# Which kind of expert unit follows which, and in what pieces the first weight blocks arrive: one change to a hybrid SSD, attention and MoE layer

## The chip, the core and the metric

The kernel runs on one core of a Trainium2 chip, as one launch. The metric is the device time in microseconds. The kernel before was timed three times: 1325.1, 1325.3 and 1327.98 us, a median of 1325.3 us. All numbers of the profile come from one further execution of it, which took 1323.47 us, with a span of 1321.8 us between its first and last instruction.

## What is computed

One layer of a streaming encoder over 512 tokens of width 1024, all in f32. The part that matters here is the end, the mixture of experts, and the very beginning, the first projection:

```python
mod = jax.nn.silu(c) @ ada_w[i] + ada_b[i]
sh1, sc1, g1, sh2, sc2, g2 = [m[:, None, :] for m in jnp.split(mod, 6, axis=-1)]
n1 = rms_norm(h, norm1_g[i]) * (1.0 + sc1) + sh1
proj = n1 @ w_in[i]            # 1024 x 6160; then SSD, banded attention, gates, w_out
...
# MoE: 64 experts (gate and up 1024x256, down 256x1024), 6 of them for each token
combine = ...                  # tokens x 64, normalised top-6 weights times 2.5
out = (jax.nn.silu(n @ s_gate) * (n @ s_up)) @ s_down
for e in range(N_EXPERTS):
    hid = jax.nn.silu(n @ e_gate[e]) * (n @ e_up[e])
    out = out + (hid @ e_down[e]) * combine[:, e:e + 1]
...
h = h + g2 * ff                # then the final rms_norm
```

Each of the 64 experts has 3 MB of weights (three transfers of 1024 KB), so the expert stage reads 192 MB.

## The kernel before

**The stages.** The input projection comes first (weights pass as blocks of 1024x256 through `ring`, a ring of four slots), then SSD, attention, the two branch projections and the gates, the output projection, the router, and the expert stage. The instructions of each engine stand in a fixed order that is written out by hand; semaphores tie the engines together.

**The first projection.** TensorE works on the first six outputs of the projection side by side (`OUTER`, 6 PSUM banks), K tile by K tile: for K tile k it does outputs 0 to 2, then the preparation of tile k+1 (`next_tile`: two tiny products of the adaLN sum of that tile, four transposes of x), then outputs 3 to 5. Outputs 0 and 1 use block 0, outputs 2 and 3 block 1, outputs 4 and 5 block 2. The preparation of a tile needs VectorE's `modulation_sum`, which in turn needs that tile's 1 MB of `ada_w` (`load_chunk`, two transfers of 512 KB). All of this is loaded by the one queue of SyncE (SP): chunk 0, the four tiles of x, then chunk 1, block 0, chunk 2, block 1, and so on.

**The expert stage.** Experts are sorted by their number of tokens on the chip. Experts 0 to 3 (`FIXED`) are taken out of the sort: their weights are loaded before the routing is known, and they are done first. The other 60 follow by rank, the fullest first. Work goes in units. In a single unit one expert has up to 128 token rows; in a pair unit two experts have 64 rows each, one in the upper and one in the lower half of the PE array's columns. The 16 fullest ranked experts (4 to 19) are singles, the rest come in pairs. The order of units before: 4 fixed singles; then 16 times single, pair; then, in a loop whose count depends on the routing (`LAST`), 6 pairs. That is 42 units here.

**Slots.** The weights sit in six slots (`gu(s)` for gate and up, `dn(s)` for down). The n-th expert in the order of use goes to slot n % 6, which the expert used six before it has left. Slots 4 and 5 first hold the normed tokens and the shared expert's weights, so their first expert loads wait for the shared expert (`sgu_ready`, `sy_ready`) and for the first gather (`gathered[0]`). SP issues each later load in the same order: it reads the expert's number from `order`, waits until the gate and up product of the slot's user is through (`gu_ready`), issues gate and up, waits until its down product is through (`ey_ready`), issues down. `unit_of` and `rank_of` turn positions into units and ranks.

**A unit on TensorE.** Gate and up (`gate_up`, line 1713), the transposes of the next unit's gathered tokens (line 1701), the down product of the unit before (`down`, line 1721), the transposes of this unit's hidden rows (line 1728). GpSimd gathers each unit's tokens from DRAM and scatters its results (lines 653 and 661) on a queue of its own; it fills one half of the row numbers from the token lists and VectorE the other (`upper`, lines 1254 and 1255).

## Time and profile before

| what | value |
|---|---|
| median of three runs | 1325.3 us |
| the profiled execution: its time, and its span | 1323.47 us, 1321.8 us |
| busy share of the span: TensorE, weight loads, VectorE, ScalarE, GpSimd | 91%, 47%, 36%, 19%, 15% |
| moved by DMA in all | 322.28 MB, mean 244 GB/s |
| SP's queue (q1), GpSimd's queue (q0) | 269.37 MB, 47.30 MB |
| first expert unit starts, last down product ends | 714.55 us, about 1270.2 us |

A busy share of 91% for TensorE hides two stretches of another kind: the first 40 us, and the expert stage from 887 us on, where it waits before many units. The rows below show them. "Idle before" in square brackets is the time that the engine stood still before the instruction, and what ended it; "issue" stands where no releaser is seen. Several instructions of a group that follow each other are merged to one row with a count. An f32 product appears as two records.

### The profile page before, as it was taken

What the parts mean: (1) busy time and instruction counts of PE and PEld (TensorE: products, weight loads), DVE (VectorE), ACT (ScalarE), POOL (GpSimd) and SP (SyncE); (2) the same over time, 40 slices, a digit from 0 to 9 for tenths busy, and PEclk for the clock granted to TensorE, in tenths of its full rate; (3) what the DMA queues carried; (4) which work ended last, traced back from release to release, by engine and by line L of the source; (5) the groups of instructions that cost most, each with busy time, mean ns of one, the idle gap of its engine ahead of it and who ended that gap; (6) DMA issues with size and microseconds to landing.
All of it is one profiled execution on the core that took longest, in us unless ns stands there. A gap on an engine that the chain in (4) does not pass through costs nothing. (4 is left out here: it accounts for less than half of the span.)

```text
span 1321.8 us, 13412 instructions
## 1 busy us (share of the span) xinstructions
PE 1203.9 (91%) x4819; PEld 619.1 (47%) x4819; DVE 471.5 (36%) x981; ACT 250.6 (19%) x615; POOL 195.9 (15%) x321
## 2 busy tenths in 40 slices
PE   3999999998999999999998999999898899978866
PEld 1545865465544444448843544433343343433322
DVE  4567035555566111113754222221222222221125
ACT  2141122133441000001122211121111111111101
POOL 4000021111002000000252122221121211111100
PEclk9999999999999998999999999999999998999988
DMA  9633232123448241137247689999999999999747
GB/s 303 179 96 95 64 128 84 61 79 128 141 131 302 64 159 32 64 105 327 80 160 271 250 337 400 422 423 421 422 411 403 410 393 410 391 406 422 306 184 288
DMA packets 108010, 322.28 MB, mean 244 GB/s; under 512 B 14405, under 2 KB 67737, under 8 KB 80937
## 3 DMA queue, kind: packets, MB, share of 16 engines
q1 hardware_dynamic: 87728, 269.37, 53.0%
q0 software_dynamic: 18688, 47.30, 10.0%
q10 hardware_dynamic: 1528, 4.77, 0.9%
q8 instruction: 38, 0.62, 0.2%
q14 instruction: 28, 0.22, 0.1%
HBM read 314.49 MB, written 26.82 MB: 258 GB/s over the span
## 5 line engine op out<-in xcount | busy, mean ns | idle before, releaser
L1713 PE MATMUL ps<-gu_hi,xsT 128*64 128x512 f32 (+1 forms) x672 | 218.4, 616 | 19.9 <-DMA gu_hi<-in_exp_w_up_dram 11.6
L1713 PEld LDWEIGHTS ps<-gu_hi,xsT 128*64 128x64 f32 (+1 forms) x672 | 84.7, 164 | 133.0 <-issue 130.6
L1271 DVE SCALAR_TENSOR_TENSOR hid<-ps,wgt,gated 128x256 f32<-128x256 f32 x42 | 20.3, 484 | 316.2 <-ACT gated L880 316.2
L1591 PE MATMUL ps<-n1T,ring 128*128 128x512 f32 x256 | 112.4, 600 | 3.7 <-DVE mod L1121 3.0
L1713 PE MATMUL ps<-gu_lo,xsT 128*64 128x512 f32 (+1 forms) x352 | 94.1, 652 | 23.1 <-issue 19.4
L1374 PE MATMUL ps<-n1T,ring 128*128 128x512 f32 x256 | 111.9, 594 | 0.0
L1721 PE MATMUL ps<-dn_hi,hidT 128*64 128x512 f32 (+1 forms) x336 | 108.6, 596 | 0.0
L661 POOL DMA_INDIRECT expert_rows<-hn,meta x42 | 41.9, 997 | 420.0 <-DVE hn L1267 397.1
L1267 DVE TENSOR_TENSOR hn<-ps,g_row 128x1024 f32<-128x1024 f32 x42 | 51.4, 1225 | 94.8 <-PE ps L1721 94.8
L1591 PEld LDWEIGHTS ps<-n1T,ring 128*128 128x128 f32 x256 | 49.1, 193 | 65.2 <-issue 61.3
L880 ACT ACTIVATE gated<-ps 128x256 f32<-128x256 f32 x42 | 16.1, 384 | 334.8 <-PE ps L1713 334.8
L1374 PEld LDWEIGHTS ps<-n1T,ring 128*128 128x128 f32 x256 | 48.1, 190 | 58.7 <-issue 58.7
L1382 PE MATMUL ps<-ring,n1T 128*128 128x256 f32 x320 | 70.3, 380 | 0.0
L870 ACT ACTIVATE xsT<-ps,mod 128x128 f32<-128x128 f32 x172 | 64.8, 457 | 26.2 <-PE ps L1701 26.2
L1713 PEld LDWEIGHTS ps<-gu_lo,xsT 128*64 128x64 f32 (+1 forms) x352 | 33.4, 154 | 75.3 <-issue 75.1
L1382 PEld LDWEIGHTS ps<-ring,n1T 128*128 128x128 f32 x320 | 60.5, 190 | 9.2 <-issue 1.2
L1721 PEld LDWEIGHTS ps<-dn_hi,hidT 128*64 128x64 f32 (+1 forms) x336 | 38.7, 160 | 47.8 <-issue 46.4
L1261 DVE TENSOR_SCALAR xsT<-ps,mod 128x128 f32<-128x128 f32 x172 | 58.8, 404 | 5.5 <-PE ps L1701 5.5
L1564 PE MATMUL ps<-xbcT,ring 128*128 128x512 f32 x128 | 58.4, 599 | 0.0
L1619 PE MATMUL ps<-ring,raw 128*128 128x256 f32 x256 | 56.6, 380 | 1.8 <-DVE raw L1111 1.8
L1701 PEld LDWEIGHTS ps<-ident,hn 128*128 128x128 f32 x344 | 42.9, 191 | 29.1 <-issue 29.1
L1591 PE MATMUL ps<-attT,ring 128*128 128x512 f32 x128 | 55.6, 592 | 0.0
(324 smaller groups left out, 1326.2 us busy)
## 6 DMA issues: line engine op xcount, KB each, us to landing
gu_hi<-in_exp_w_gate_dram SPq DMA_DIRECT2D x42, 1024.0 KB, 14.9
gu_hi<-in_exp_w_up_dram SPq DMA_DIRECT2D x42, 1024.0 KB, 26.5
dn_hi<-in_exp_w_down_dram SPq DMA_DIRECT2D x42, 1024.0 KB, 24.9
ring<-in_w_in_dram SPq DMA_DIRECT2D x24, 1024.0 KB, 5.7
gu_lo<-in_exp_w_gate_dram SPq DMA_DIRECT2D x22, 1024.0 KB
gu_lo<-in_exp_w_up_dram SPq DMA_DIRECT2D x22, 1024.0 KB
dn_lo<-in_exp_w_down_dram SPq DMA_DIRECT2D x22, 1024.0 KB
h<-in_ada_w_dram POOLq DMA_DIRECT2D x32, 512.0 KB, 4.9
```

Of the source, the lines that this page charges most:

```text
L661: pool.indirect_dma_start(out=rows_d[:, :], out_offset=bass.IndirectOffsetOnAxis(ap=meta[:, c, 1:2], axis=0), in_=ys[:, b, :], in_offset=N ...
L870: ins = act.activation(xsT[:, b, k, :], ps[:, 0, P * k:P * k + P], ACT.Identity, bias=B2[:, k:k + 1], scale=A2[:, k:k + 1])
L1261: ins = dve.tensor_scalar(xsT[:, b, k, :], ps[:, 1, P * (k - 4):P * (k - 4) + P], A2[:, k:k + 1], B2[:, k:k + 1], ALU.mult, ALU.add)
L1267: dve.tensor_tensor(ys[:, b, :], flat(ps[:, 5:7, :]), g2_row[:, :], ALU.mult).then_inc(ey_dve, 1)
L1374: ins = pe.matmul(bank, w[:, k, lo:lo + P], n1T[:, k, :], start=(k == 0), stop=(k == KC - 1))
L1382: ins = pe.matmul(bank[:, 0:WB], n1T[:, k, P * t:P * t + P], w[:, k, :], start=(k == 0), stop=(k == KC - 1))
L1564: ins = pe.matmul(ps[:, 1, :], w[:, k, P * (m % 2):P * (m % 2) + P], uT[:, k, :], start=(k == 0), stop=(k == KC - 1))
L1591: ins = pe.matmul(ps[:, 4 * jj + b, :], w[:, k, P * jj:P * jj + P], src[:, k, :], start=(k == 0), stop=(k == KC - 1))
L1619: ins = pe.matmul(ps[:, 2 * (t % 2) + b // 2, WB * (b % 2):WB * (b % 2) + WB], mergedT[:, k, P * t:P * t + P], w[:, k, :], start=(k == 0), ...
L1701: ins = pe.transpose(ps[:, k // 4, P * (k % 4):P * (k % 4) + P], xs[:, b, :].rearrange("p (f k) -> p k f", k=KC)[:, k, :], ident[:, :])
L1713: ins = pe.matmul(ps[rows, 2 + b, :], xsT[:, b, k, rows], gu(s)[:, :, k, :], start=(k == 0), stop=(k == KC - 1))
L1721: ins = pe.matmul(ps[rows, 5 + half, :], hidT[:, jj, rows], dn(s)[:, jj, BANK * half:BANK * half + BANK], start=(jj == 0), stop=(jj == 1))
```

## The change

Three things are changed.

1. The order of the units. Now a pair follows each of the four fixed singles, and then come 4 times single, pair, single, pair, single, single, pair. The six pairs of the loop stay. There are 42 units as before, with the same experts in singles and in pairs: pairs still start with rank 20 and singles with rank 4. The slots are no longer n % 6 by position but come from a table (`SLOT`): the i-th expert to be loaded takes the slot of the expert that was used i-6-th. For a pair, SP now reads both numbers, waits once for `gu_ready`, issues gate and up of both experts, waits once for `ey_ready`, and issues both down loads; before, the second expert's gate and up stood behind the first one's wait for `ey_ready`.
2. The first three weight blocks are loaded in pieces by K tile: tile 0 of all three, then tiles 1 and 2, then tiles 3 to 7 (`PARTS`, `load_rows`), between the chunks 0, 1 and 2 of `ada_w`. TensorE waits for a piece of all three blocks at K tiles 0, 1 and 3. Block 3 is loaded behind the last chunk.
3. Since the second unit is now a pair of ranked experts, its first gather needs `order`. GpSimd's wait for it moves ahead of the first two gathers, and VectorE fills the row numbers of the first three units before the shared expert's third hidden tile (`shared_hid(2)`) and no longer behind it.

```diff
-BEFORE = FIXED + 2 * PAIRED
 SEQ0 = FIXED + 3 * PAIRED
+KINDS = "FP" * FIXED + "SPSPSSP" * (PAIRED // 4)
+BEFORE = len(KINDS)
...
+def plan():
+    ranks = {"F": iter(range(FIXED)), "S": iter(range(FIXED, SINGLES)), "P": iter(range(SINGLES, SEQ0))}
+    units = [[next(ranks[kind]) for _ in range(1 + (kind == "P"))] for kind in KINDS]
+    used = [r for unit in units for r in unit] + list(range(SEQ0, NE))
+    loads = list(range(FIXED)) + [r for r in used if r >= FIXED]
+    slot, nth, refill = {}, {}, [[] for _ in units]
+    for i, r in enumerate(loads):
+        slot[r] = i if i < SLOTS else slot[used[i - SLOTS]]
+        nth[r] = 1 + sum(slot[q] == slot[r] for q in loads[:i])
+        if i >= SLOTS and r < SEQ0:
+            refill[[used[i - SLOTS] in unit for unit in units].index(True)].append(r)
+    return units, slot, nth, refill, loads[FIXED:SLOTS]
...
+    PARTS = [slice(0, 1), slice(1, 3), slice(3, KC)]
...
+            def load_rows(part):
+                ks = PARTS[part]
+                for n in range(OUTER // 2):
+                    w, col = blocks[n]
+                    sp.dma_start(ring[:, n, ks, :], w[:, ks, col:col + WB]).then_inc(w_slot[part], 16)
...
-            for k in range(1, KC):
+            load_rows(0)
+            load_chunk(1)
+            load_rows(1)
+            load_chunk(2)
+            load_rows(2)
+            for k in range(3, KC):
                 load_chunk(k)
-                if k <= RING:
-                    load_block(k - 1)
+            load_block(OUTER // 2)
...
-            for n in range(SLOTS, SEQ0):
-                e = sp.value_load(order[0:1, rank_of(n):rank_of(n) + 1], min_val=0, max_val=NE - 1)
-                sp.wait_ge(gu_ready, unit_of(n - SLOTS) + 1)
-                load_gu(n % SLOTS, e)
-                sp.wait_ge(ey_ready, unit_of(n - SLOTS) + 1)
-                load_dn(n % SLOTS, e)
+            for un in range(BEFORE):
+                ids = [expert(r) for r in REFILL[un]]
+                if ids:
+                    sp.wait_ge(gu_ready, un + 1)
+                    for r, e in zip(REFILL[un], ids):
+                        load_gu(SLOT[r], e)
+                    sp.wait_ge(ey_ready, un + 1)
+                    for r, e in zip(REFILL[un], ids):
+                        load_dn(SLOT[r], e)
...
+            pool.wait_ge(ordered, ORDER)
             for un in range(2):
                 gather(un % 6, un % 2, lower(un), 2 * (un + 1))
...
-            pool.wait_ge(ordered, ORDER)
...
             shared_hid(1)
-            shared_hid(2)
+            dve.wait_ge(ordered, ORDER)
             dve.wait_ge(lists_in, 32)
             for un in range(3):
-                upper(un, NE + un)
+                upper(un, upper_column(un))
+            shared_hid(2)
...
+            first_rows = {ks.start: part for part, ks in enumerate(PARTS)}
...
-                    w = block_in(j // 2)
+                    w = ring[:, j // 2, :, :]
+                    if j == 0 and k in first_rows:
+                        pe.wait_ge(w_slot[first_rows[k]], 16 * OUTER // 2)
```

The same on the engines. First SP's queue at the start of the program, of the kernel before (`xbcT`, `siluz` and `attT` lend their room to the chunks of `ada_w`, `h` to x):

```order
L401 DMA xbcT<-in_ada_w_dram 128x8x128 x2
L406 DMA h<-in_x_dram 128x1024 x4
L401 DMA xbcT<-in_ada_w_dram 128x8x128 x2
L397 DMA ring<-in_w_in_dram 128x8x256
L401 DMA xbcT<-in_ada_w_dram 128x8x128 x2
L397 DMA ring<-in_w_in_dram 128x8x256
L401 DMA siluz<-in_ada_w_dram 128x8x128 x2
L397 DMA ring<-in_w_in_dram 128x8x256
L401 DMA siluz<-in_ada_w_dram 128x8x128 x2
L397 DMA ring<-in_w_in_dram 128x8x256
```

And the same place now:

```order
L409 DMA xbcT<-in_ada_w_dram 128x8x128 x2
L414 DMA h<-in_x_dram 128x1024 x4
L405 DMA ring<-in_w_in_dram 128x256 x3
L409 DMA xbcT<-in_ada_w_dram 128x8x128 x2
L405 DMA ring<-in_w_in_dram 128x2x256 x3
L409 DMA xbcT<-in_ada_w_dram 128x8x128 x2
L405 DMA ring<-in_w_in_dram 128x5x256 x3
L409 DMA siluz<-in_ada_w_dram 128x8x128 x4
```

K tile 0 of the three blocks has moved ahead of chunk 1, and block 2's first tile no longer stands behind chunk 3.

Next, SP's queue behind the down load of slot 5 in the expert stage, before: the refills behind units 0 and 1 (`TENSOR_LOAD` reads an expert's number; `ISA` are register instructions).

```order
L462 TENSOR_LOAD order
L462 ISA x2
L439 ISA
L439 DMA gu_hi<-in_exp_w_gate_dram 128x2048
L440 DMA gu_hi<-in_exp_w_up_dram 128x2048
L443 DMA dn_hi<-in_exp_w_down_dram 128x2048
L462 TENSOR_LOAD order
L462 ISA x2
L439 ISA
L439 DMA gu_hi<-in_exp_w_gate_dram 128x2048
L440 DMA gu_hi<-in_exp_w_up_dram 128x2048
L443 DMA dn_hi<-in_exp_w_down_dram 128x2048
```

And now, the refill behind unit 1:

```order
L465 TENSOR_LOAD order
L465 ISA x2
L465 TENSOR_LOAD order
L465 ISA x2
L451 ISA
L451 DMA gu_hi<-in_exp_w_gate_dram 128x2048
L452 DMA gu_hi<-in_exp_w_up_dram 128x2048
L451 ISA
L451 DMA gu_hi<-in_exp_w_gate_dram 128x2048
L452 DMA gu_hi<-in_exp_w_up_dram 128x2048
L455 DMA dn_hi<-in_exp_w_down_dram 128x2048 x2
```

Unit 1, a pair now, frees two slots at once, and four loads of gate and up stand ahead of the two of down.

Last, VectorE at the passage from the shared expert to the first units, before (`hid` is the shared expert's hidden tile, `meta` and `wgt` the row numbers and weights of a unit):

```order
L1213 TENSOR_TENSOR hid<-ps,gated 128x256 x2
L1254 CAST meta<-lists 64x2
L1255 COPY wgt<-lists 64x1
L1254 CAST meta<-lists 64x2
L1255 COPY wgt<-lists 64x1
L1254 CAST meta<-lists 64x2
L1255 COPY wgt<-lists 64x1
```

And now:

```order
L1230 TENSOR_TENSOR hid<-ps,gated 128x256
L1271 CAST meta<-lists 64x2
L1272 COPY wgt<-lists 64x1
L1295 TENSOR_LOAD order
L1295 ISA x2
L1271 ISA
L1271 COPY meta<-lists 64x2
L1272 ISA
L1272 COPY wgt<-lists 64x1
L1271 CAST meta<-lists 64x2
L1272 COPY wgt<-lists 64x1
L1230 TENSOR_TENSOR hid<-ps,gated 128x256
```

The row numbers now stand between the second and the third hidden tile, and those of unit 1 are found through a read of `order`.

## Rows read from the trace of the kernel before

**Rows 1.** The page: busy tenths and DMA rate in 40 slices of the span.

```profile
PE   3999999998999999999998999999898899978866
...
GB/s 303 179 96 95 64 128 84 61 79 128 141 131 302 64 159 32 64 105 327 80 160 271 250 337 400 422 423 421 422 411 403 410 393 410 391 406 422 306 184 288
```

**Rows 2.** Timeline, TensorE, 19 to 51 us: start, length, engine, line, idle before.

```profile
19.66 3.78 PE L1410 MATMUL ps<-n1T,ring 128*128 128x512 f32 x4 [0.94 <-ACT n1T L719]
...
25.97 1.30 PE L1410 MATMUL ps<-n1T,ring 128*128 128x512 f32 x2 [2.53 <-DMA ring<-in_w_in_dram]
...
32.60 6.25 PE L1410 MATMUL ps<-n1T,ring 128*128 128x512 f32 x10 [2.14 <-DMA ring<-in_w_in_dram]
38.69 0.50 PE L1395 MATMUL ps<-ones,btok 128*128 128x1 f32 x4
...
39.53 5.32 PE L1410 MATMUL ps<-n1T,ring 128*128 128x512 f32 x12
...
50.66 0.50 PE L1395 MATMUL ps<-ones,btok 128*128 128x1 f32 x4
```

**Rows 3.** Timeline, VectorE's sum of tile 1 and SP's queue.

```profile
18.78 3.68 DVE L932 SCALAR_TENSOR_TENSOR cb<-xbcT,small,cb 128x256 f32<-128x256 f32 x7
...
19.23 3.69 SPq L401 DMA_DIRECT2D siluz<-in_ada_w_dram  x2
...
22.97 2.78 SPq L397 DMA_DIRECT2D ring<-in_w_in_dram  x1
```

**Rows 4.** Windows: busy by engine, TensorE's clock, DMA share, GB/s last.

```profile
720.00:740.00 20.00, 18.86 (x59) 9.43 (x58) 5.27 (x15) 4.44 (x12) 2.90 (x7) 1.00 0.53 202
740.00:810.00 70.00, 70.00 (x247) 32.41 (x246) 19.72 (x48) 13.65 (x36) 14.59 (x25) 1.00 0.89 342
...
1020.00:1030.00 10.00, 8.27 (x38) 3.07 (x40) 2.84 (x8) 1.89 (x5) 2.36 (x4) 1.00 0.91 364
```

**Rows 5.** Timeline, gate and up of units 5 to 7, and of two late pairs.

```profile
770.02 7.09 PE L1713 MATMUL ps<-gu_hi,xsT 128*64 128x512 f32 x32
...
781.69 7.03 PE L1713 MATMUL ps<-gu_hi,xsT 128*128 128x512 f32 x16
...
793.55 7.09 PE L1713 MATMUL ps<-gu_lo,xsT 128*64 128x512 f32 x32
...
945.26 8.62 PE L1713 MATMUL ps<-gu_lo,xsT 128*64 128x512 f32 x32 [3.66 <-issue]
...
1052.87 8.78 PE L1713 MATMUL ps<-gu_lo,xsT 128*64 128x512 f32 x32 [3.54 <-issue]
```

**Rows 6.** Timeline, SP's queue, 699 to 738 us.

```profile
699.38 0.36 SPq L439 DMA_DIRECT2D gu_hi<-in_exp_w_gate_dram  x1
...
721.86 0.33 SPq L439 DMA_DIRECT2D gu_hi<-in_exp_w_gate_dram  x1
...
735.66 0.33 SPq L443 DMA_DIRECT2D dn_hi<-in_exp_w_down_dram  x1
736.74 0.33 SPq L439 DMA_DIRECT2D gu_hi<-in_exp_w_gate_dram  x1
```

**Rows 7.** Timeline, passage to the units, 693 to 715 us.

```profile
693.66 0.42 DVE L1213 TENSOR_TENSOR hid<-ps,gated 128x256 f32<-128x256 f32 x1 [3.98 <-PE ps L1684]
...
695.16 1.70 POOL L653 DMA_INDIRECT hn<-norm_rows,meta  x1 [5.60 <-DVE wgt L1255]
...
699.29 1.13 PE L1701 MATMUL ps<-ident,hn 128*128 128x128 f32 x8 [0.81 <-DMA hn<-norm_rows,meta]
...
702.29 5.40 PE L1694 MATMUL ps<-dn_hi,hidT 128*128 128x512 f32 x8 [1.63 <-ACT hidT L840]
...
714.55 7.13 PE L1713 MATMUL ps<-gu_hi,xsT 128*128 128x512 f32 x16 [1.17 <-ACT hn L848]
```

**Rows 8.** The page: DMA issues of up, KB each, median us to landing.

```profile
gu_hi<-in_exp_w_up_dram SPq DMA_DIRECT2D x42, 1024.0 KB, 26.5
```

**Rows 9.** Timeline, the last down product.

```profile
1266.57 3.65 PE L1721 MATMUL ps<-dn_lo,hidT 128*64 128x512 f32 x16 [1.15 <-DVE hn L1267]
```

More of the change, by code:

```diff
@@ L65 @@
 UNTIL_MERGED = 700
[L68 to L87 removed]
+def plan():
[10 more added lines that the diff above has]
+    return units, slot, nth, refill, loads[FIXED:SLOTS]
+UNITS, SLOT, NTH, REFILL, FIRST = plan()
 def hybrid_ssd_swa_moe_adaln_block(nc, a):
@@ L451, in _, with expert @@
             sp.wait_ge(ordered, ORDER)
-            ids = [sp.value_load(order[0:1, rank_of(n):rank_of(n) + 1], min_val=0, max_val=NE - 1)
-                   for n in (FIXED, FIXED + 1)]
+            def expert(r):
+                return sp.value_load(order[0:1, r:r + 1], min_val=0, max_val=NE - 1)
+            ids = [expert(r) for r in FIRST]
             sp.wait_ge(sgu_ready, T)
@@ L471, in _ @@
                                          max_val=EMPTY) & (NE - 1) for i in range(2)]
-                    slots = [(SEQ0 + 2 * m + i) % SLOTS for i in range(2)]
+                    slots = [SLOT[SEQ0 + 2 * m + i] for i in range(2)]
                     for i in range(2):
@@ L640, in lower @@
             def lower(un):
-                return un if un < FIXED else pool.value_load(order[0:1, rank_of(experts_of(un)[0]):rank_of(experts_of(un)[0]) + 1],
-                                                           min_val=0, max_val=NE - 1)
+                r = UNITS[un][0]
+                return r if r < FIXED else pool.value_load(order[0:1, r:r + 1], min_val=0, max_val=NE - 1)
             def from_table(j, m):
@@ L1356, in block_in @@
             def block_in(n):
-                pe.wait_ge(w_slot[n % RING], 16 * (n // RING + 1))
+                pe.wait_ge(w_slot[n % RING], 16 * (n // RING + (1 if n % RING == RING - 1 else OUTER // 2)))
                 return ring[:, n % RING, :, :]
@@ L1767, in _ @@
             for un in range(BEFORE):
-                for n in experts_of(un):
-                    pe.wait_ge(gu_in[n % SLOTS], 32 * (n // SLOTS + 1))
+                for r in UNITS[un]:
+                    pe.wait_ge(gu_in[SLOT[r]], 32 * NTH[r])
                 pe.wait_ge(exT_act, un + 1)
@@ L1773, in _ @@
                     pe.wait_ge(hid_done, un - 1)
-                gate_up(un % 2, [n % SLOTS for n in experts_of(un)])
+                gate_up(un % 2, [SLOT[r] for r in UNITS[un]])
                 turn_in((un + 1) % 2, 16 * ((un + 1) // 2 + 1))
@@ L1779, in _ @@
                         pe.wait_ge(ey_dve, un - 1)
-                    for n in experts_of(un - 1):
-                        pe.wait_ge(dn_in[n % SLOTS], 16 * (n // SLOTS + 1))
-                    down([n % SLOTS for n in experts_of(un - 1)])
+                    for r in UNITS[un - 1]:
+                        pe.wait_ge(dn_in[SLOT[r]], 16 * NTH[r])
+                    down([SLOT[r] for r in UNITS[un - 1]])
                 hidden_T(un + 1)
-            pairs = [[(SEQ0 + 2 * m + i) % SLOTS for i in range(2)] for m in range(LAST)]
+            pairs = [[SEQ0 + 2 * m + i for i in range(2)] for m in range(LAST)]
+            previous = [UNITS[BEFORE - 1]] + pairs[:LAST - 1]
             count = load_turns(pe)
@@ L1788, in _ @@
                     at = j * LAST + (BEFORE + m)
-                    for i in range(2):
-                        pe.wait_ge(gu_in[pairs[m][i]], j * (32 * 2 * LAST // SLOTS) + 32 * ((SEQ0 + 2 * m + i) // SLOTS + 1))
+                    for r in pairs[m]:
+                        pe.wait_ge(gu_in[SLOT[r]], j * (32 * 2 * LAST // SLOTS) + 32 * NTH[r])
                     pe.wait_ge(exT_act, at + 1)
@@ L1793, in _ @@
                     pe.wait_ge(hid_done, at - 1)
-                    gate_up(m % 2, pairs[m])
+                    gate_up(m % 2, [SLOT[r] for r in pairs[m]])
                     turn_in((m + 1) % 2, j * (16 * LAST // 2) + 16 * ((BEFORE + m + 1) // 2 + 1))
@@ L1797, in _ @@
                     pe.wait_ge(ey_dve, at - 1)
-                    for i in range(2):
-                        pe.wait_ge(dn_in[pairs[m - 1][i]], j * (16 * 2 * LAST // SLOTS) + 16 * ((SEQ0 + 2 * m - 2 + i) // SLOTS + 1))
-                    down(pairs[m - 1])
+                    for r in previous[m]:
+                        pe.wait_ge(dn_in[SLOT[r]], j * (16 * 2 * LAST // SLOTS) + 16 * NTH[r])
+                    down([SLOT[r] for r in previous[m]])
                     hidden_T(at + 1)
@@ L1804, in _ @@
             pe.wait_ge(ey_dve, units - 1)
-            for i in range(2):
-                pe.wait_ge(dn_in[pairs[LAST - 1][i]], count * (16 * 2 * LAST // SLOTS) + 16 * ((SEQ0 - 2 + i) // SLOTS + 1))
-            down(pairs[LAST - 1])
+            for r in pairs[LAST - 1]:
+                pe.wait_ge(dn_in[SLOT[r]], count * (16 * 2 * LAST // SLOTS) + 16 * (NTH[r] - 2 * LAST // SLOTS))
+            down([SLOT[r] for r in pairs[LAST - 1]])
             pe.to_reg(units)
```

22 lines of the change are left out of this document (4 added, 18 removed).

## The prediction

> **What bounds the kernel now.** I read the 40 slices first [rows 1]. A slice is 33 us. TensorE is at 9 or 8 tenths nearly everywhere but in the first slice and the last; the DMA rate is mostly under 330 GB/s up to 760 us and near 422 from 826 on. So there are two places where something other than TensorE's own work can set the time: the start, and the expert stage, where both are nearly full. The middle (60 to 690 us) I take to be TensorE's own pace; a shift of the start moves it as a whole.
>
> Then the timeline of the start [rows 2]. The first K tile's products begin at 19.66 us, wait 2.53 us for block 1 (25.97) and 2.14 us more for block 2 (32.60). Only then does TensorE go on, at a steady period: the preparation of one tile comes at 38.69 and that of the next but one at 50.66, which is 5.98 us for each tile, with no wait. The start is bound by the order of transfers, up to 32.60.
>
> Then the expert stage by windows and units. From 740 to 810 TensorE never waits (70.00 busy of 70), and the DMA rate climbs: 202 GB/s at 720 to 740, 342 at 740 to 810 [rows 4], then 422, 423, 421, 422 in slices of 33 us [rows 1]. 422 is what the queues reach at best. Later TensorE waits ahead of pairs, 3.66 us at 945.26 and 3.54 us at 1052.87 [rows 5]. A pair takes TensorE hardly longer than a single: 781.69 - 770.02 = 11.67 us for the pair at 770, 793.55 - 781.69 = 11.86 for the single behind it, but a pair frees and needs 6.3 MB of weights, a single 3.15. So before, the stage first has five singles in a row in which TensorE is slower than the DMA, which runs below its rate since no slot is free; then it is bound by the DMA: from 945.26 to 1052.87 are 8 units with 12 experts in 107.6 us, which is 13.5 us for a unit, against 11.8 of TensorE's own. What is lost is the DMA's capacity early on.
>
> **The change part by part.**
>
> *The blocks in pieces.* The transfers of 1 MB cost the queue, by the time that SP is held at the issue, 3.69 us for a chunk and 2.78 us for a block [rows 3]. Block 2 lands at 32.60 before [rows 2], behind chunks 0 to 3, x, and blocks 0 and 1. In the new order chunk 3 is the last of the very same set of bytes, so chunk 3 lands at 32.6 and everything else earlier: tile 0 of the blocks about 1 us behind x, and chunk 2 ahead of block 1's old 25.97, since only 3/8 + 6/8 = 1.125 blocks stand in front of it instead of 2: 0.875 x 2.78 = 2.4 us, so at 23.5. TensorE: tile 0 starts at 19.66 as before, three outputs take half of 5.32 us, 2.66. Preparation of tile 1: VectorE's sum of it ends at 22.46 [rows 3], so at 22.5. Sum of tile 2 from about 23.5 to 27.6; TensorE is there at 22.5 + 0.84 + 5.32 = 28.6. Sum of tile 3 waits for chunk 3 at 32.6 and takes 4.0 (the seven operations of 3.68 us and one ahead of them), to 36.6. So the preparation that stood at 38.69 + 5.98 = 44.7 now stands at 36.6, a gain of 8.1 us; the next is at 36.6 + 0.84 + 5.32 = 42.8 instead of 50.66, 7.9 us. From there on TensorE is the slowest again (VectorE's sum is 4.0 us and a chunk's transfer 3.7, under TensorE's 5.98). Term: **8.0 us less**. Bounds: without the wait for chunk 3 the preparation of tile 2 would be at 28.6 instead of 38.69, so 10.1 at most; and if each of the six transfers more costs the queue what two transfers of 512 KB cost over one of 1 MB, 3.69 - 2.78 = 0.9 us, chunk 3 lands 5.5 us later and 2.5 us are left. I take 8.0, since the chunk's higher price is as well explained by its shorter rows (512 bytes against 1 KB in a block), and the pieces keep the rows of the block. Block 3, now behind chunk 7, lands near 50 us and is needed only after the last K tile; its cover is some 20 us.
>
> The Trainium skill, "DMA: Bandwidth & Descriptors", section "Bandwidth", speaks against this part: it wants transfers of at least 1 MiB for three quarters of the peak, and the pieces of tile 0 are 128 KB. By the fit in its section "Anatomy of one DMA" (2.0 us and the bytes at 436 GB/s, for GpSimd's path) six more transfers would be an estimated 12 us if their fixed parts came one behind the other, and the gain of the start would be gone. Here the trace disagrees as far as it shows: the two transfers of a chunk hold SP for 3.69 us together, less than the fixed parts alone would be.
>
> *The passage to the units.* Before, the row numbers of units 0 to 2 stand behind the third hidden tile, which starts at 693.66 for want of a transpose; the first gather goes out at 695.16 and TensorE waits 0.81 us for it at 699.29 [rows 7]. Now they follow the second tile, with the lists in at about 689.3 (the gather's GpSimd had waited 5.60 us for VectorE [rows 7]). The read of `order` is new on VectorE and GpSimd; SP shows 1.08 us from a down issue of 735.66 to the next gate issue at 736.74 [rows 6], less 0.33 for the issue, so 0.7 us for such a read. Even with it the third tile comes in time for its transposes, which stand behind that wait, and the gather lands by about 695 to 696, when TensorE is still in the shared expert. Term: **0.8 us less**. Bounds: 0, if ScalarE's evacuations set the pace there; 2.4, if the 1.63 us for ScalarE ahead of the product at 702.29 go with the 0.81. GpSimd's wait for `order` is met long before. SP's loads for slots 4 and 5 start some 4 us sooner than 699.38; nothing needs them sooner.
>
> *The order of units.* Unit 1 is a pair in slots 4 and 5. Their loads begin at 699.38 before [rows 6] and some 4 us earlier now; five loads, 5.2 MB, at 422 GB/s are 12.4 us, so they land by about 714 and are needed at about 723: no wait. Unit 0 frees one slot at 721.86, unit 1 two slots at about 736. From then on the four F, P couples ask, in 23.5 us (11.67 + 11.86), for 3 experts, 9.44 MB, and two gathers and scatters. From 945.26 to 1052.87 12 experts make 37.7 MB of 107.6 us x 410 GB/s = 44.1 MB (410 as the mean of the slices there, 422, 411, 403, 410 [rows 1]), so gather and scatter are 0.80 MB for a unit. That is 11.1 MB in 23.5 us, or 473 GB/s, over the 422 that the queues can do. So the DMA is full from about 736 on instead of 810.
>
> Is unit 3 (second pair) in time? Its second expert's gate and up go out at 736.7, behind one down load, with the queue nearly empty: 3 MB ahead and in it, 7.5 us at 422, and about 2 us to land, so 746 to 747, and unit 3 begins at 747. It is just in time; a wait of 1 us would cost nothing in the end, since the DMA sets it.
>
> Worth: from 740 to 810 before, 70 us at 422 - 342 = 80 GB/s are 5.6 MB unused, or 13.3 us at 422; the end of the stage is DMA-bound, so it comes earlier by this, less what the new order leaves unused later. Before, the rate falls in a window like 1020 to 1030 to 364 GB/s, (422 - 364) x 10 / 422 = 1.4 us lost, about once in 50 us. New are four places with two singles in a row, where TensorE frees 2 slots in 23.5 us; I put a loss of 0.8 us on each (over half of such a dip, since a backlog from the pair ahead covers the rest), 3.3 in all. Term: **10 us less**. Bounds: 13.3 above; below, 3 us, if each of the four places costs a whole dip and the queue fills only at 760, one couple later (24 x 80 / 422 = 4.5 us given back; 13.3 - 4.5 - 4 x 1.4). The earlier issue of a pair's second gate and up is in this: in the DMA-bound part it changes only the order in the queue.
>
> *Sum.* 8.0 + 0.8 + 10 = 18.8 us. From the profiled execution's 1323.47 that is 1304.7; the median of the runs, 1325.3, lies 1.8 us above that execution. Forecast **1306.5 us**.
>
> **The rivals.**
>
> - *The order of units gives nothing.* The stage stays DMA-bound at both ends and every byte saved early is given back at the double singles and ahead of the last six pairs. For it: before, too, the DMA is not full between 1020 and 1140. Against it: the demand in the mixed part (28 units of 11.8 us, 330 us, for 40 experts, 126 MB, and 28 x 0.80 = 22 MB) is 148 MB, 351 us at 422, so the DMA stays the slower one. Time: 1325.3 - 8.8 = 1316.5.
> - *The pieces cost a fixed time each.* Six more transfers at 0.9 us, the gain of the start is 2.5: 1306.5 + 5.5 = 1312. This is the rule of the page cited above in the kernel's own prices. A chunk's two transfers speak for 0.9 at most.
> - *More than forecast.* The queue never empties (13.3), chunk 3 comes a microsecond sooner (9), the passage 2.4: 1325.3 - 24.7, about 1300.5.
> - *Pairs too early, slower than before.* Units 3, 5 and 7 are pairs whose second expert is asked for only one unit (11.4 us) ahead. If it lands not after 9 but after the median of 26.5 us [rows 8], each waits 26.5 - 10.7 = 15.8 us (10.7 from 736.7 to unit 3's start), three times 47 us, and TensorE frees slots later by as much. The later waits of before would go, 13.5 - 11.8 = 1.7 us for each of the 20 units up to the loop in which the DMA sets the pace, 34 us; the start's 8.8 stays: 1325.3 + 47 - 34 - 8.8 = 1329.5. It decides from (34 + 8.8) / 3 = 14.3 us of wait for each such pair. Against it: 26.5 us is the time through a queue with 9 MB in it; at 720 to 740 the rate is 202 GB/s, the queue is short.
> - *The change does not reach the time*: waits of the middle absorb the start and the order does nothing, 1325.
>
> **How the numbers follow.** Forecast as above 0.57, its own range 1301 to 1312; order of units gives nothing 0.14; pieces cost 0.11; more than forecast 0.10; pairs too early 0.05; no effect 0.03. A difference of 0.2% (2.7 us) is about what a measurement of this kernel can tell from none. Faster: 0.57 + 0.14 + 0.11 + 0.10 = 0.92; same 0.03; slower 0.05. Range for 8 in 10: 1298 to 1318, which takes in the first two rivals and half of the third.
>
> **What would show it.** In the changed kernel: no wait for `ring` in K tile 0, and TensorE's preparation of tile 4 near 42.8 us instead of 50.66; the wait for chunk 3 at 32.6 on VectorE. The first unit starts near 714.55 - 8.8 = 705.7 [rows 7]. From there 22 to 96 us behind the first unit's start (740 to 810 before) the DMA rate is over 410 GB/s instead of 342. No wait before units 3, 5 and 7 of over 1 us. The last down product ends near 1270.2 [rows 9] - 18.8 = 1251.4. I am wrong if the DMA rate there stays under 400, if the start saves under 5 us, or if the mixed part shows windows under 370 GB/s more often than before.

## The result, and the profile after

The changed kernel takes 1308.7 us (median of 4 runs, 1307.3 to 1309.7), the kernel before 1325.2 beside it (4 runs, 1322.2 to 1328.0). The ratio is 0.9875, its 95% interval 0.9852 to 0.9899. The forecast was 1306.5. The profiled execution took 1308.93 with a span of 1306.7, 15.1 us less than the span before.

The page of the changed kernel, TensorE's busy tenths, its granted clock and the DMA rate in 40 slices of 32.7 us, against [rows 1]:

```profile
PE   5999999998999999999998999998988999988866
...
PEclk9999999999999998999999999998998999999988
...
GB/s 299 188 129 64 74 152 67 97 33 129 157 125 299 65 161 33 65 98 329 62 190 280 304 423 421 423 423 418 420 407 395 410 394 413 353 415 406 273 186 285
```

Both places that the prediction named have moved. TensorE's first slice goes from 3 to 5 tenths. The DMA is at 423 GB/s in the 24th slice (before, the 24th had 337 and the 25th 400). New is the 353 in the 35th slice, just ahead of the loop with the last six pairs.

The start, TensorE's timeline of the changed kernel (start, length, engine, line, idle before), against [rows 2]; line 1410 is now 1431, line 1395 is 1413:

```profile
19.56 5.38 PE L1431 MATMUL ps<-n1T,ring 128*128 128x512 f32 x6 [0.93 <-ACT n1T L736]
24.77 0.50 PE L1413 MATMUL ps<-ones,cb 128*128 128x1 f32 x4
...
25.60 5.32 PE L1431 MATMUL ps<-n1T,ring 128*128 128x512 f32 x12
30.75 0.50 PE L1413 MATMUL ps<-ones,btok 128*128 128x1 f32 x4
...
37.35 0.61 PE L1413 MATMUL ps<-ones,cb 128*128 128x1 f32 x4 [0.45 <-DVE cb L949]
...
43.44 0.50 PE L1413 MATMUL ps<-ones,btok 128*128 128x1 f32 x4
```

and VectorE's, where it waits for chunk 3:

```profile
33.30 0.35 DVE L947 TENSOR_SCALAR cb<-siluz,small 128x256 f32<-128x256 f32 x1 [1.72 <-DMA siluz<-in_ada_w_dram]
33.69 3.61 DVE L949 SCALAR_TENSOR_TENSOR cb<-siluz,small,cb 128x256 f32<-128x256 f32 x7
```

The products no longer wait for `ring`. The preparation that stood at 50.66 stands at 43.44: 7.2 us. Chunk 3 is let through at 33.30, not at 32.6.

The passage to the units, TensorE's timeline, against [rows 7] (line 1701 is now 1722, 1694 is 1715, 1713 is 1734):

```profile
692.96 1.04 PE L1722 MATMUL ps<-ident,hn 128*128 128x128 f32 x8
...
695.90 3.70 PE L1715 MATMUL ps<-dn_hi,hidT 128*128 128x512 f32 x8 [1.66 <-ACT hidT L857]
```

The transposes of the first unit don't wait for their gather. The wait for ScalarE ahead of the product is still there (1.66, before 1.63), but that product takes 3.70 us where it took 5.40 [rows 7].

The windows that answer to [rows 4] (busy by engine, granted clock, DMA share, GB/s last); 736 to 802 lies as far behind the first unit as 744 to 810 before, whose row comes last:

```profile
728.00:736.00 8.00, 8.00 (x28) 4.05 (x28) 1.94 (x5) 0.86 (x3) 2.36 (x4) 1.00 0.88 310
736.00:802.00 66.00, 66.00 (x261) 28.14 (x257) 19.17 (x47) 13.13 (x35) 13.07 (x23) 1.00 1.02 419
...
1120.00:1130.00 10.00, 10.00 (x39) 4.53 (x38) 3.28 (x8) 2.27 (x6) 1.31 (x3) 1.00 0.91 361
1130.00:1140.00 10.00, 8.25 (x27) 4.13 (x25) 3.28 (x8) 2.27 (x6) 1.04 (x1) 1.00 0.79 310
```

```profile
744.00:810.00 66.00, 66.00 (x232) 30.08 (x231) 18.90 (x47) 12.90 (x35) 13.76 (x24) 1.00 0.88 338
```

419 where 338 stood, and two low windows in a row ahead of the loop. Over the whole stretch that the prediction named, 22 to 96 us behind the first unit (728 to 802 here), the mean is 407, since the queue fills up only at 736. Followed from start to end, in us of the span (starts of instructions in the two timelines; units are counted from 0):

| | before | after | earlier by |
|---|---|---|---|
| start: preparation of tile 4 | 50.66 | 43.44 | 7.2 |
| last tile's eight transposes (`turn_u`) | 307.98 | 301.12 | 6.9 |
| first product group behind them | 311.78 | 306.53 | 5.3 |
| first unit, gate and up | 714.55 | 706.47 | 8.1 |
| unit 35, the last ahead of the loop | 1158.46 | 1140.59 | 17.9 |
| unit 41, the last | 1253.22 | 1236.50 | 16.7 |
| last down product | 1266.57 | 1251.46 | 15.1 |

The last down product ends at 1255.1; the forecast had 1251.4. Each line of the table is a question: why 7.2 at the start, where 1.6 of it went at 301 us, why the passage gave 2.8, and why the 9.8 won from unit 0 to unit 35 are 7.0 at the end.

### The profile page after: what moved, and what is told of

Same layout as the page of the kernel before. It is cut to its first block, busy times and chain, and to the rows that moved or that the text cites. A ratio compares the mean times of both kernels' runs of the same rounds, so it can differ in the third digit from the quotient of the medians.

```text
span 1306.7 us, 13414 instructions
## 1 busy us (share of the span) xinstructions
PE 1201.0 (92%) x4819; PEld 619.3 (47%) x4819; DVE 472.1 (36%) x981; ACT 250.1 (19%) x615; POOL 196.1 (15%) x321
## 4 chain that ended last, share of the span: by engine, by line
PE 78%; DMA 8%; DVE 6%; issue 3%; SPq 3%; ACT 1%; POOL 0%; POOLq 0%; DVEq 0%; ACTq 0%
PE ps L1734 19%; PE ps L1612 13%; PE ps L1742 9%; PE ps L1392 7%; DMA gu_lo<-in_exp_w_up_dram 7%; PE ps L1400 4%; PE ps L1640 4%; PE ps L1722 3%; PE ps L1585 2%; PE ps L1431 2%; PE ps L1840 2%; PE ps L1695 2%; DVE seg L1032 1%; PE ps L1715 1%; PE ps L1549 1%
## 5 line engine op out<-in xcount | busy, mean ns | idle before, releaser
L1734 PE MATMUL ps<-gu_hi,xsT 128*64 128x512 f32 (+1 forms) x704 | 247.9, 623 | 23.5 <-issue 11.0
L1734 PE MATMUL ps<-gu_lo,xsT 128*64 128x512 f32 (+1 forms) x320 | 152.6, 633 | 13.6 <-issue 6.7
L1742 PE MATMUL ps<-dn_hi,hidT 128*64 128x512 f32 (+1 forms) x352 | 119.9, 597 | 1.1 <-DVE hn L1284 1.1
L1734 PEld LDWEIGHTS ps<-gu_lo,xsT 128*64 128x64 f32 (+1 forms) x320 | 52.6, 170 | 67.8 <-issue 67.1
L1742 PE MATMUL ps<-dn_lo,hidT 128*64 128x512 f32 (+1 forms) x160 | 72.5, 596 | 0.0
```

What stands on the lines that cost most here:

```text
L1734: ins = pe.matmul(ps[rows, 2 + b, :], xsT[:, b, k, rows], gu(s)[:, :, k, :], start=(k == 0), stop=(k == KC - 1))
L1742: ins = pe.matmul(ps[rows, 5 + half, :], hidT[:, jj, rows], dn(s)[:, jj, BANK * half:BANK * half + BANK], start=(jj == 0), stop=(jj == 1))
```

## The experiments

### One part at a time

Three kernels, each the kernel before with one part of the change. They and the next ran against 1325.0 us (16 runs of the kernel before).

**The pieces alone.** In the kernel before:

```diff
-            for k in range(1, KC):
-                load_chunk(k)
-                if k <= RING:
-                    load_block(k - 1)
+            load_rows(0)
+            load_chunk(1)
+            load_rows(1)
+            load_chunk(2)
+            load_rows(2)
+            ...
```

> The kernel before with the first three weight blocks in pieces by K tile, nothing else. If the start's gain is passed on in full to the end (theory A): about 7 us less than before (the trace of the changed kernel has tile 4's preparation at 43.44 us instead of 50.66), ratio 0.9945. If the middle or the DMA-bound expert stage absorbs it (theory B): under 2 us less. Either way the first tile has no wait for ring. The first expert unit would start at 707 to 708 us by A, since the passage is as before.

Measured: 1317.7 (1316.3 to 1319.6), ratio 0.9947, 0.9929 to 0.9965. That is 7.3 us by the medians (4.6 to 9.4 by the interval) and what the start's own timeline shows: as far as this can tell, it is passed on whole. First unit at 708.03, 6.5 sooner; from unit 0 to unit 41 539.2 us, before 538.7. Nine pieces of 128 to 640 KB in the place of three of 1 MB cost the queue no more than the 0.7 us by which chunk 3 is late. By the rule of the Trainium skill's page "DMA: Bandwidth & Descriptors", section "Bandwidth", that transfers want at least 1 MiB for three quarters of the peak, the pieces should have cost the queue dearly. This kernel does not bear it out for a queue in which the transfers stand one behind the other.

**The row numbers of units 0 to 2 ahead of the third hidden tile, alone.**

```diff
             shared_hid(1)
-            shared_hid(2)
             dve.wait_ge(lists_in, 32)
             for un in range(3):
                 upper(un, NE + un)
+            shared_hid(2)
```

> The kernel before with VectorE's row numbers of the first three units ahead of the shared expert's third hidden tile, nothing else. Theory A: the wait of 0.81 us for the first gather goes, and the product behind the following wait of 1.63 us runs in 3.70 us instead of 5.40 with the clock kept, so the first unit starts 2.5 us sooner, ratio 0.998. Theory B: the 1.7 us belong to the phase in which the clock happened to be and not to the edit, so 0.8 us or less, not to be told from none.

Measured: 1322.1 (10 runs, 1318.3 to 1323.9), ratio 0.9969, 0.9953 to 0.9984. By the medians that is 2.9 us, by the ratio 4.1 (2.1 to 6.2); my bound was 2.4. TensorE's timeline of this kernel:

```profile
694.94 3.70 PE L1694 MATMUL ps<-dn_hi,hidT 128*128 128x512 f32 x8 [1.22 <-ACT hidT L840]
698.48 1.05 PE L1701 MATMUL ps<-ident,hn 128*128 128x128 f32 x8
699.36 0.40 PE L1684 MATMUL ps<-ident,hid 128*128 128x128 f32 x2
701.42 3.70 PE L1694 MATMUL ps<-dn_hi,hidT 128*128 128x512 f32 x8 [1.66 <-ACT hidT L840]
```

The product behind the transposes starts 0.87 us sooner than at 702.29 [rows 7], which is the wait that went, and is 1.70 us shorter, since it runs at the full clock: 2.57 together, and the first unit stands at 711.99, 2.56 sooner. The price of the wait of 0.81 us was three times the wait. Theory B, that the 1.7 us were chance, can be held against the other profiles: the product at this place takes 5.40 and 5.34 us in the two kernels whose wait for the gather is 0.81 and 0.89 us (the kernel before and the pieces alone), and 3.70 us in the other eleven, ten of them without that wait and one with 0.20 us of it.

**The order of the units alone** (the slot table, the kinds and the joint refill; start and passage as before, but for the waits and reads of `order` on GpSimd and VectorE, which the new second unit needs):

```diff
+KINDS = "FP" * FIXED + "SPSPSSP" * (PAIRED // 4)
```

> The changed kernel with the start and the passage as before: only the order of units, the table of slots and SP's common refill of a pair. Theory A (early DMA capacity used): the stretch from the first unit to the last down product is 7 to 10 us shorter than the 555.7 us of before, the run 7 to 10 us shorter, ratio 0.994; the DMA rate from 22 to 96 us behind the first unit is over 400 GB/s. Theory B (the order gives nothing, the gain comes from the earlier start): under 2 us less.

Measured: 1314.7 (1313.5 to 1316.2), ratio 0.9915, 0.9883 to 0.9947: 10.3 us. From unit 0 to unit 41 530.2 us, 8.5 less than before. The window from 744 to 810, as far behind the first unit as the one above, has 420 GB/s. The three parts alone add to 20.5 us, together they give 16.5. The difference is within the intervals (that of the order alone is 8 us wide). Part of it is counted twice: in the profile of the order alone the wait for the first gather is 0.20 us and the product behind it takes 3.70, so its passage too is 2.3 us shorter than before. And where the granted clock drops differs from one profiled execution to the next, as is shown below.

**The changed kernel, a refill of two slots one slot at a time.**

```diff
-                    sp.wait_ge(gu_ready, un + 1)
                     for r, e in zip(REFILL[un], ids):
+                        sp.wait_ge(gu_ready, un + 1)
                         load_gu(SLOT[r], e)
-                    sp.wait_ge(ey_ready, un + 1)
-                    for r, e in zip(REFILL[un], ids):
+                        sp.wait_ge(ey_ready, un + 1)
                         load_dn(SLOT[r], e)
```

> The changed kernel, but SP refills a pair's slots one after the other again: gate and up, wait for the down product, down, then the second expert's. Theory A (the order of units is what counts): within 2 us of the changed kernel, a unit such as the second pair waits some 0 to 3 us for its second expert. Theory B (the common refill carries the gain, since the second expert's gate and up leave 11 us sooner): 5 us or more slower than the changed kernel, with waits before units 3, 5 and 7.

Measured: 1309.1 (1307.0 to 1310.5), ratio 0.987. From unit 0 to unit 41 531.9 us against 530.0; no difference in the time that this measurement can tell, and no wait ahead of units 3, 5 and 7. That a pair's second gate and up go out ahead of its downs is worth 1.9 us in these two profiles; the interval of the time (0.9838 to 0.9901) is too wide to say more.

### What in the order pays, and what takes it back

Four changes to the changed kernel, against 1326.3 (7 runs of the kernel before).

**No pairs behind the resident singles; they come last instead.**

```diff
-KINDS = "FP" * FIXED + "SPSPSSP" * (PAIRED // 4)
+KINDS = "F" * FIXED + "SPSPSSP" * (PAIRED // 4) + "PPPP"
```

> The changed kernel with the order FFFF, SPSPSSP x4, PPPP: the resident experts stand alone again, the four pairs that followed them stand ahead of the loop. Theory A (the gain is the DMA capacity behind the resident experts): the stage is about as long as before the change, 8 to 10 us longer than in the changed kernel, time near 1317 to 1320, DMA rate under 360 GB/s from 22 to 96 us behind the first unit. Theory B (the mixing of singles and pairs gives it): within 3 us of the changed kernel.

Measured: 1314.6 (1314.1 to 1315.1), ratio 0.9921, 0.9897 to 0.9945. From unit 0 to unit 41 537.3 us, only 1.4 less than before: the mixing of singles and pairs is worth that, the early pairs 7.2. The rate of under 360 GB/s is what theory A said. Its time, 1317 to 1320, was missed, and so was theory B's: the kernel is 5.8 us over the changed kernel's 1308.7, not 8 to 10 and not within 3. The window, and where the missing transfers are paid for:

```profile
728.00:802.00 74.00, 74.00 (x256) 34.22 (x255) 20.72 (x51) 13.80 (x37) 16.17 (x28) 1.00 0.92 351
```

```profile
1117.26 8.21 PE L1734 MATMUL ps<-gu_hi,xsT 128*64 128x512 f32 x30 [8.10 <-issue]
```

**The loop's first refill one unit sooner.** SP waits ahead of the loop for unit 33, though unit 32 has freed the slots.

```diff
+                    used_by = j * LAST + (BEFORE - SLOTS // 2 + m + 1) if m else j * (LAST + 1) + (BEFORE - SLOTS // 2)
-                    sp.wait_ge(gu_ready, j * LAST + (BEFORE - SLOTS // 2 + m + 1))
+                    sp.wait_ge(gu_ready, used_by)
```

> The changed kernel, but SP loads the loop's first pair of experts (in its first round) behind unit 32, which frees the slots, and not behind unit 33. In the changed kernel's trace the DMA rate falls to 361 and 310 GB/s from 1120 to 1140 us, which is 4.1 us of queue time at 422. Theory A (the end of the stage is bound by DMA, so any queue time won comes back): 3 to 4 us less than the changed kernel, no window under 370 there. Theory B (the slots behind it are the limit, the dip only moves): under 1 us.

Measured: 1307.5 (1304.9 to 1309.3), ratio 0.9871, 0.9844 to 0.9898. The dip at 1120 to 1140 is gone, but it comes back 20 us later:

```profile
1120.00:1130.00 10.00, 10.00 (x40) 4.48 (x39) 3.28 (x8) 2.27 (x6) 2.22 (x4) 1.00 1.01 417
1130.00:1140.00 10.00, 7.45 (x27) 3.71 (x27) 3.27 (x8) 2.27 (x6) 1.45 (x4) 0.98 1.00 406
1140.00:1150.00 10.00, 10.00 (x43) 4.42 (x40) 1.28 (x4) 1.18 (x4) 1.04 (x1) 0.85 0.92 379
1150.00:1160.00 10.00, 8.99 (x39) 3.45 (x39) 2.02 (x5) 1.10 (x4) 2.35 (x4) 1.00 0.80 317
```

where the changed kernel has:

```profile
1140.00:1150.00 10.00, 9.41 (x38) 3.85 (x39) 0.18 (x1) 0.38 (x1) 2.35 (x4) 0.83 1.00 396
1150.00:1160.00 10.00, 8.22 (x35) 3.56 (x35) 3.12 (x8) 1.89 (x5) 2.34 (x4) 1.00 1.02 423
```

From 1120 to 1160 the mean is 380 GB/s, in the changed kernel 373: hardly more was moved. The way from unit 0 to unit 36 is only 0.9 us shorter (448.5 instead of 449.4), the loop's five periods are the same 80.7 us (80.6), and the time is the same within its error. This is theory B: the dip only moves. What a gap of the queue costs that is really closed, this run doesn't show.

**Twelve times a single and a pair, then four singles ahead of the loop.**

```diff
-KINDS = "FP" * FIXED + "SPSPSSP" * (PAIRED // 4)
+KINDS = "FP" * FIXED + "SP" * 12 + "SSSS"
```

> The changed kernel with the order FP x4, SP x12, SSSS in place of FP x4, SPSPSSP x4: the four double singles are gone, four singles stand ahead of the loop. Theory A, by the prediction's 0.8 us for each double single: the mixed part itself gains up to 3 us, but four singles in a row ahead of the loop free one slot per 11.7 us and the loop's first load waits for the second of them, so the DMA rate falls under 350 there for some 20 us; in all 0 to 4 us slower than the changed kernel. Theory B (double singles are the cost and nothing else is): 3 us faster.

Measured: 1305.7 (1304.8 to 1306.2), ratio 0.9855, 0.9831 to 0.9879; 528.6 us from unit 0 to unit 41. This order has singles in a row only at its end, and its queue is emptier ahead of the loop than any:

```profile
1110.00:1120.00 10.00, 10.00 (x35) 4.95 (x35) 2.82 (x7) 1.68 (x5) 2.36 (x4) 1.00 0.80 320
1120.00:1130.00 10.00, 10.00 (x35) 4.22 (x32) 1.91 (x5) 1.00 (x4) 2.36 (x4) 1.00 0.46 184
```

and is no slower: 3.0 us under the changed kernel's 1308.7 and 1.2 under its second measurement (below). It reaches unit 36 2.5 us later behind unit 0 (451.9 us, 449.4 in the changed kernel), but with its slots full: no wait ahead of unit 36, 0.53 us ahead of unit 37, and the loop's first five units take 76.7 us instead of 80.6. So the 2.5 us are won back in the loop. It is no rule that an idle queue with full slots is free: behind the first unit the kernel before has just that, and there it costs the 7.2 us above.

**The last tile's filling job whole ahead of its transposes**, to cover the wait at 301 us in the middle, behind which 1.6 us were lost (below).

```diff
-                fill(last, range(KC // 2))
+                cut = KC if t == T - 1 else KC // 2
+                fill(last, range(cut))
                 turn_u(t)
-                fill(last, range(KC // 2, KC))
+                if cut < KC:
+                    fill(last, range(cut, KC))
```

> The changed kernel, but for the last of the four SSD tiles TensorE does the whole filling job ahead of turn_u, not half of it. In the traces it waits 3.17 us there for VectorE, and in the changed kernel the transposes and the products behind the wait take 1.97 + 2.73 us instead of 1.16 + 1.89 at the lower clock. Half a job is 1.9 us. Theory A: the wait shrinks to 1.3 us and the clock stays high, 1.9 to 3.5 us less than the changed kernel. Theory B (the clock's fall there is chance and VectorE sets the pace of what follows): 0 to 1 us less.

Measured: 1306.9 (1305.3 to 1308.2), ratio 0.9866, 0.9841 to 0.9891. Its timeline:

```profile
300.66 1.16 PE L1518 MATMUL ps<-ident,h 128*128 128x128 f32 x8 [1.44 <-DVE h L1065]
```

The wait is 1.44 us instead of 3.17 and the clock holds, but another of 1.41 for VectorE follows at 303.23. First unit at 704.92; in the changed kernel 706.47 and, profiled again (below), 705.30. In the time that is within the error.

### What is left, and all three small edits at once

Three kernels against 1325.4 (9 runs of the kernel before). First the changed kernel itself again:

> The changed kernel itself, beside the next two on one chip. Both theories: 1308.7, within 1.5 (its earlier runs lay between 1307.3 and 1309.7).

Measured: 1306.9 (1305.3 to 1308.6), ratio 0.9863, 0.9845 to 0.9881. The same kernel stood at 1308.7 in the first measurement; so 1.8 us lie between two measurements of it, 0.3 more than I had allowed. Differences of 1 to 3 us between the kernels here are of that size. Its profile has the first unit at 705.30, 1.2 sooner than the other profile.

**Half of each refill's gate and up.** This kernel leaves out K tiles 4 to 7 of gate and up in each refill; its products read what the slot held, so its output isn't the layer's. It is only there to be timed.

```diff
+            def load_half(s, e):
+                sp.dma_start(gu(s)[:, 0, 0:KC // 2, :], which(w_gate, e)[:, 0:KC // 2, :]).then_inc(gu_in[s], 16)
+                sp.dma_start(gu(s)[:, 1, 0:KC // 2, :], which(w_up, e)[:, 0:KC // 2, :]).then_inc(gu_in[s], 16)
...
-                        load_gu(SLOT[r], e)
+                        load_half(SLOT[r], e)
...
-                        load_gu(slots[i], ids[i])
+                        load_half(slots[i], ids[i])
```

> The changed kernel, in which every gate/up load of a slot's refill moves only four of the eight K tiles (the products read old data in the other four): the bytes of a refill go from 3 to 2 parts of 3, and all products stay. Theory 1 (what is left of waiting in the unit stage is the transfer of the weights): the waits of pairs go, the period of the loop's pairs falls from 16.1 to the time of the products themselves, 11.67 and 3.65 make 15.3, and that of a single and a pair from some 24.9 to 22.4 at full clock (7.13 + 3.6 + 11.67 is this sum); the stage is some 25 shorter, 1284, between 1275 and 1292. Theory 2 (the rows gathered and scattered on GpSimd's queue set the period): they stay as they are, the period stays at 16.1, and the time is within 3 of the changed kernel's.

Measured: 1258.9 (1255.3 to 1259.3), ratio 0.9493, 0.9473 to 0.9513: 48 us faster than the changed kernel, nearly twice my figure. The products of a unit take 11.8 us, not 15.3: I had added the down product (3.65) to 11.67, which already holds it. The direction tells the theories apart all the same. The groups of gate and up products between 700 and 1260 us, busy time and mean ns of one, then idle before, of the changed kernel:

```profile
L1734 PE MATMUL ps<-gu_hi,xsT 128*64 128x512 f32 (+1 forms) x704 | 247.9, 623 | 23.5 <-issue 11.0 <-DMA gu_hi<-in_exp_w_up_dram 6.0 <-DMA gu_lo<-in_exp_w_up_dram 4.2
L1734 PE MATMUL ps<-gu_lo,xsT 128*64 128x512 f32 (+1 forms) x320 | 152.6, 633 | 13.6 <-issue 6.7 <-DMA gu_hi<-in_exp_w_up_dram 6.6 <-DMA gu_lo<-in_exp_w_up_dram 0.4
```

and of the one with half the bytes:

```profile
L1738 PE MATMUL ps<-gu_hi,xsT 128*64 128x512 f32 (+1 forms) x704 | 233.3, 595 | 2.3 <-ACT hn L869 1.2 <-ACT xsT L891 1.1
L1738 PE MATMUL ps<-gu_lo,xsT 128*64 128x512 f32 (+1 forms) x320 | 141.2, 594 | 0.0
```

From unit 0 to unit 41 it takes 480.9 us, the changed kernel 530.0. Of these 49.1 us, 34.9 are the waits ahead of the changed kernel's units 2 to 41, added up in its timeline. Another 13.0 are six gate/up groups that take 8.7 to 10.0 us in the place of 7.09, each right behind a wait of 2.3 to 4.4 us (a seventh, unit 41's own, lies behind this stretch and costs 1.6 more); with half the bytes there is neither. Both go with the bytes. Gathers and scatters are the same in both kernels, so they don't set the period.

**The three small edits together** (four singles ahead of the loop, its first refill one unit sooner, the filling job whole).

> The changed kernel with the three single edits together: twelve times a single and a pair and then four singles ahead of the loop, the loop's first refill one unit sooner, and the last tile's filling job whole ahead of its eight transposes. Theory 1 (their gains lie in different places and are real): each alone was 1.3 to 3.1 faster than the changed kernel's median, with intervals that overlap; together 1303.5, between 1301.5 and 1305.5. Theory 2 (the stage is held by the bytes of the weights, and what was seen was the play of the granted clock): 1306 to 1309, no less than the best of the three alone, 1305.7.

Measured: 1304.9 (5 runs, 1304.5 to 1305.6), ratio 0.9849, 0.9835 to 0.9863. It has the lowest median of the kernels that do the whole work, 2.0 us under the changed kernel's measured beside it, at the edge of what can be told; its parts don't add up (the four singles alone have 1305.7). Against the changed kernel's profile taken beside it its first unit is 0.6 us sooner (704.66), the way to unit 41 is the same (529.5 and 529.6), and unit 41's gate and up take 7.09 us instead of 8.78: 2.4 us, which is the difference of the spans (1302.8 and 1305.2). Theory 1's range holds the time, but the gain doesn't lie where it said: the larger part is clock, which theory 2 named. Whether this order keeps the clock more often is likely, as all five runs have a mean clock of 0.976 to 0.978 against 0.972 or 0.973 of the changed kernel's four, and not shown beyond that.

## Why the prediction was right

**The start** (8.0 forecast, bounds 2.5 to 10.1): 7.2 in the timeline, 7.3 measured alone. There is no wait for `ring`, the sum of tile 3 stands behind chunk 3, and the preparation of tile 4 comes near 42.8 (43.44). One step in between was wrong and did not show: the first three outputs were given 2.66 us, the steady pace, and take 5.38; [rows 2] has 3.78 us for two of them, so this could have been read there. The preparations of tiles 1 and 2, forecast at 22.5 and 28.6, come at 24.77 and 30.75. The wait for chunk 3 covers this, by luck and just so: ahead of the preparation of tile 3 TensorE waits only 0.45 us. The upper bound of 10.1 rested on the 28.6; 38.69 less 30.75 leaves 7.9. The rival in which each piece costs a fixed time is out: chunk 3 would have come at 38.1 and came at 33.3.

**That a shift of the start moves the middle as a whole** seems to fail in the table: 6.9 us at the last transposes, 5.3 behind them. TensorE waits the same 3.17 us there in both. In the kernel before:

```profile
307.98 1.16 PE L1497 MATMUL ps<-ident,h 128*128 128x128 f32 x8 [3.17 <-DVE h L1048]
308.98 1.89 PE L1382 MATMUL ps<-ring,n1T 128*128 128x256 f32 x8
```

and in the changed kernel, with the window behind it (granted clock third from the end):

```profile
301.12 1.97 PE L1518 MATMUL ps<-ident,h 128*128 128x128 f32 x8 [3.17 <-DVE h L1065]
302.89 2.73 PE L1400 MATMUL ps<-ring,n1T 128*128 128x256 f32 x8
```

```profile
300.00:306.00 6.00, 4.50 (x16) 3.67 (x16) 2.11 (x3) 0.71 (x2) 2.31 (x5) 0.72 0.20 38
```

1.97 + 2.73 against 1.16 + 1.89: 1.65 us go to the clock behind the same wait. But this is most likely no doing of the change. In the kernel before with only the row numbers moved, whose start is the old one, the same place reads:

```profile
307.10 1.97 PE L1497 MATMUL ps<-ident,h 128*128 128x128 f32 x8 [3.17 <-DVE h L1048]
308.87 2.46 PE L1382 MATMUL ps<-ring,n1T 128*128 128x256 f32 x8
```

All ten other profiles in which this wait of 3.17 us stands (3.18 in one) show products above their full-clock length behind it. The profile of the kernel before is the one that kept its clock there, and its execution was 1.8 us under its median. So the spans (15.1) understate the gain a little, and the medians (16.5) are the fairer measure.

**The passage** (0.8, bounds 0 to 2.4): 2.8 in the traces, 2.9 measured alone. This is the term that was mis-sized most in proportion. The step that fell short was the price of the wait: the 0.81 us was priced at 0.81. What stands behind a wait is part of its price: the product at 702.29 took 5.40 us [rows 7] against the 3.70 of its sisters, and I had that row before me. The 5.40 should have been read as 3.70 and 1.70 of the lower clock; 0.8 + 1.7 = 2.5 is what came. That the first unit, forecast at 705.7, stands at 706.47 is partly luck: the 2.0 us more in the passage nearly cancel the 1.6 lost in the middle and the 0.8 less at the start.

**The order of units** (10, bounds 3 to 13.3): 9.8 by unit 35, 8.6 by unit 41, 7.0 to the last down product; 10.3 alone in the time. The mechanism held: 419 GB/s from 736 on, no wait ahead of units 3, 5 and 7, and the kernel without the early pairs loses 7.2 of 8.6 again. Two of the prediction's own signs came out on the edge: over its whole stretch the rate is 407, not over 410, and between 800 us and the loop four windows of 10 us lie under 370 GB/s (360, 354, 361, 310) where the kernel before has three (364, 353, 337). By unit 35 the size is right. Two things were not foreseen: 0.8 us just ahead of the loop, where unit 36 follows unit 35 after 15.31 us, 14.49 before; and the last unit's gate and up, 8.72 us where it took 7.09 before, 1.6 us. The first was sized at double singles only, 0.8 a place; that the queue runs low ahead of the loop too, where the slots' own order of refills changes, was left out. That the order gives nothing is out (its chance was 0.14), and so is the slower case: a pair's second expert landed in time, as the queue was short.

**The sum**: 18.8 forecast, 16.5 measured by the medians and 15.1 by the spans. By the spans: 7.2 at the start, less 0.3 up to 301 us and 1.6 at it, 2.8 in the passage, 7.0 in the stage. Against the forecast that is 0.8 less at the start, 1.9 lost in the middle, 2.0 more in the passage and 3.0 less in the stage. Of what is missing, 1.65 at 301 us and 1.6 in the last unit are clock that the one execution before kept and the one after did not.

**What stays open**: in which executions the clock drops behind a wait of 2 to 4 us; no run here controls it. And no run closes the queue's gap ahead of the loop without opening another, so what it costs is not known.

## What to carry to other kernels

Where a first product waits for a whole block, load the first blocks by K tile across all outputs, in the order in which they are used: six transfers more cost this queue, which is kept busy, at most 0.7 us. Where a stage goes from compute-bound to transfer-bound, look for the stretch in which the queue is not full and put the units that free and need the most there. Price a wait on TensorE with the product behind it, at both clock levels.

## What the hardware showed

- A wait of TensorE can cost more than itself: the 0.81 us at 699.29 us cost 2.57. In the changed kernel's unit stage, gate and up of a pair at the granted clock of 2.4 GHz take 7.09 us; in groups that run partly at 1.2 GHz 8.7 to 10.0 (the granted clock is 0.73 from 896 to 907 us, around the one of 9.39). With no waits in the unit stage the clock is 1.00 in every window of 100 us from 730 to 1130, where the changed kernel has 0.97 to 1.00.
- The same wait does not always do so: behind the 3.17 us ahead of the last transposes the clock held in one profile of eleven. With four singles ahead of the loop a wait of 2.80 us was followed by 8.78 us of gate and up, and one of 2.76 us by 7.09, in one execution:

```profile
937.38 8.78 PE L1734 MATMUL ps<-gu_hi,xsT 128*64 128x512 f32 x32 [2.80 <-issue]
...
991.37 7.09 PE L1734 MATMUL ps<-gu_hi,xsT 128*64 128x512 f32 x32 [2.76 <-issue]
```

- A pair of experts costs TensorE about what a single costs: with half the bytes the period is 11.5 to 11.9 us for either in the units 2 to 35. Only the bytes tell them apart.
- The loop's pairs follow each other by 16.0 to 16.6 us (the last by 15.4), each behind a wait for its weights, in the changed kernel and the kernel before, and by 12.1 with half the gate and up.
